# Output stage: the first tile's matmuls walk the 128-row blocks of the weight for both column halves, the second tile's low part is made before the row loads are waited for, and the gate row is loaded by itself

## The reference, cut to what matters

```python
o = jnp.concatenate([o_r, o_h], axis=-1)          # mixer output, 1056 x 1024
mix = o @ W_out                                   # W_out is 1024 x 1024
x = x + gt1 * mix                                 # gate row, one per sequence
h = rmsnorm(x, norm2_g) * (1 + sc2) + sh2         # scale row and shift row
ff = hier_moe(h, ...)                             # router logits of h choose 2 of 16 experts
x = x + gt2 * ff
```

## Time and profile before

| | us |
|---|---|
| median of three runs | 1271.62 |
| the profiled execution, its own time | 1272.07 |
| its span | 1270.3 |
| output stage, from about 656.5 to 832.0 | 175.5 |
| PE busy in that stage | 135.27 |
| DVE busy in that stage | 111.60 |
| ACT busy in that stage | 42.41 |

### The profile page before, as it was taken

How to read it: one execution, slowest core, us unless ns; L and a number is a source line. 1 busy time by engine, 2 the same in 40 slices (tenths; PEclk the granted TensorE clock), 3 DMA queues, 4 the chain that set the end, 5 groups by cost and what they waited for, 6 DMA issues and landing times. The chain is left out here.

```text
span 1270.3 us, 26353 instructions
## 1 busy us (share of the span) xinstructions
PE 1076.6 (85%) x8764; PEld 894.3 (70%) x8765; DVE 717.3 (56%) x1328; ACT 605.9 (48%) x1219; POOL 113.2 (9%) x237
## 2 busy tenths in 40 slices
PE   4689998999989999899948999439999998999800
PEld 4688787977888788877836877337877776777600
DVE  3523555146622565235654675767896684767359
ACT  5634445344543445334551221156786574767334
POOL 0000000000000000000000011220011011111042
PEclk9699999999999999999968999669999999999955
DMA  8532222042122221123225341288999896999175
GB/s 335 183 89 72 77 80 68 26 138 81 38 64 68 80 80 50 44 77 109 80 90 181 101 149 58 75 276 314 373 390 346 303 355 206 375 301 375 70 257 195
DMA packets 202261, 210.63 MB, mean 166 GB/s; under 512 B 15596, under 2 KB 169060, under 8 KB 201892
## 3 DMA queue, kind: packets, MB, share of 16 engines
q1 hardware_dynamic: 182976, 177.25, 41.9%
q0 software_dynamic: 5712, 18.23, 4.1%
q10 hardware_dynamic: 13492, 13.96, 3.1%
HBM read 185.32 MB, written 24.08 MB: 165 GB/s over the span
## 5 line engine op out<-in xcount | busy, mean ns | idle before, releaser
L1998 DVE TENSOR_TENSOR experts_w_lo<-all_raw,experts_w_hi 128x2048 fp32r<-128x2048 f32 x48 | 109.5, 2284 | 6.5 <-ACT experts_w_hi L1879 6.5
L1998 DVE TENSOR_TENSOR experts_w_lo<-experts_raw_more,experts_w_hi 128x2048 fp32r<-128x2048 f32 x48 | 108.3, 2287 | 8.4 <-ACT experts_w_hi L1879 8.4
L908 PE MATMUL early_ps_proj<-mixers_w_hi,early_h_hi 128*128 128x512 f32 x256 | 106.4, 416 | 2.6 <-ACT mixers_decay L741 2.6
L2165 PE MATMUL experts_ps_g<-experts_w_hi,experts_x_hi 128*128 128x512 f32 x256 | 104.4, 408 | 2.2 <-DVE experts_x_lo L2004 2.2
L910 PE MATMUL early_ps_proj<-mixers_w_hi,early_h_lo 128*128 128x512 f32 x256 | 101.1, 395 | 0.0
L2167 PE MATMUL experts_ps_g<-experts_w_hi,experts_x_lo 128*128 128x512 f32 x256 | 100.7, 393 | 0.0
L909 PE MATMUL early_ps_proj<-mixers_w_lo,early_h_hi 128*128 128x512 f32 x256 | 100.6, 393 | 0.0
L2166 PE MATMUL experts_ps_g<-experts_w_lo,experts_x_hi 128*128 128x512 f32 x256 | 100.5, 393 | 0.0
L1198 DVE TENSOR_TENSOR mixers_qd_t<-mixers_turned,early_tables 128x128 f32<-128x128 f32 (+1 forms) x36 | 10.1, 281 | 153.1 <-ACT mixers_turned L789 135.8
L1879 ACT ACTIVATE experts_w_hi<-all_raw 128x2048 fp32r<-128x2048 f32 x48 | 91.5, 1910 | 6.8 <-DMA all_raw<-in_W_up_e_dram 3.5
L1879 ACT ACTIVATE experts_w_hi<-experts_raw_more 128x2048 fp32r<-128x2048 f32 x48 | 91.6, 1913 | 2.2 <-DMA experts_raw_more<-in_W_up_e_dram 1.1
(11 more groups left out here) (354 smaller groups left out, 2757.7 us busy)
## 6 DMA issues: line engine op xcount, KB each, us to landing
experts_raw_more<-in_W_down_e_dram SPq DMA_DIRECT2D x128, 256.0 KB, 5.0
all_raw<-in_W_gate_e_dram SPq DMA_DIRECT2D x96, 256.0 KB, 5.5
all_raw<-in_W_up_e_dram SPq DMA_DIRECT2D x96, 256.0 KB, 6.8
all_raw<-in_W_in_dram SPq DMA_DIRECT2D x32, 512.0 KB, 4.6
all_raw<-in_W_ada_dram SPq DMA_DIRECT2D x32, 512.0 KB, 5.4
condition_w_ada_in<-in_W_ada_dram SPq DMA_DIRECT2D x4, 2048.0 KB, 12.4
experts_raw_more<-in_W_gate_e_dram SPq DMA_DIRECT2D x32, 256.0 KB, 7.2
experts_raw_more<-in_W_up_e_dram SPq DMA_DIRECT2D x32, 256.0 KB, 7.4
```

Source lines behind the costliest of these rows:

```text
L908: pe.matmul(out, xhi, whi, start=(k == 0), stop=False)
L1998: dve.tensor_tensor(w_lo[:, 2 * p:2 * p + 2], raw_pair[p], f32(w_hi[:, 2 * p:2 * p + 2]), ALU.subtract).then_inc(lo_done, 1)
L2165: pe.matmul(out, x_hi[:, k, :], w_hi[:, c, at], start=(k == 0), stop=False)
```

## The change

On SP the load of `o` tile 1 is issued right behind that of tile 0. The gate row of the prompt becomes a load of its own (512 KB) that counts on `x_in[0]`, the semaphore of the even x tiles; the shift and the scale row follow in one load (1024 KB) on `rows_in`. `o` tile 2 and x tile 1 are issued before the tile loop; the sample's rows, with their wait, come behind them. In the loop, the loads of turn 0 are gone, since they were made earlier. On PE, tile 0 takes the blocks k outside and the two column halves inside; all other tiles keep their order. On DVE the low part of tile 1 comes right behind the weights, ahead of the wait for the rows; the making of (1 + scale) * gain, with the wait for `rows_in`, is put behind the x addition of tile 0 for the prompt and behind that of tile 3 for the sample; the wait for the router's loads moves to turn 1, ahead of the first use of the bias.

```diff
             o_tile(0)
-
+            o_tile(1)
             for k in range(6, KD):
                 sp.wait_ge(lo_done, k - 5)
                 sp.dma_start(raw[:, W_OUT_AT[k]], a["W_out"][0, k * P:(k + 1) * P, :])\
                   .then_inc(raw_in[k - 6], 16)
             x_tile(0)
-            o_tile(1)
-            for q, rows in ((0, P), (1, DEC)):
-                if q == 1:
-                    sp.wait_ge(lo_done, KD)
-                sp.dma_start(mod[q][0:rows], s.mod_scr[q:q + 1, 0:3 * D].rearrange("o (c d) -> o c d", c=3)
-                             .broadcast_to([rows, 3, D])).then_inc(rows_in, 16)
+            mod_row = lambda q: s.mod_scr[q:q + 1, 0:3 * D].rearrange("o (c d) -> o c d", c=3)
+            sp.dma_start(mod[0][:, 0:1], mod_row(0)[:, 0:1].broadcast_to([P, 1, D])).then_inc(x_in[0], 16)
+            o_tile(2)
+            sp.dma_start(mod[0][:, 1:3], mod_row(0)[:, 1:3].broadcast_to([P, 2, D])).then_inc(rows_in, 16)
             sp.dma_start(gain[:, :], a["norm2_g"].broadcast_to([P, D])).then_inc(rows_in, 16)
+            x_tile(1)
+            sp.wait_ge(lo_done, KD)
+            sp.dma_start(mod[1][0:DEC], mod_row(1).broadcast_to([DEC, 3, D])).then_inc(rows_in, 16)
...
-                if i + 2 < NT:
+                if 0 < i < NT - 2:
                     o_tile(i + 2)
-                if i + 1 < NT:
+                if 0 < i < NT - 1:
                     x_tile(i + 1)
...
-                for c in range(2):
-                    for k in range(KD):
+                order = [(c, k) for c in range(2) for k in range(KD)] if i else [(c, k) for k in range(KD) for c in range(2)]
+                for c, k in order:
                         if i == 0 and c == 0:
                             pe.wait_ge(lo_done, k + 1)
...
-                    last.then_inc(mm_done, 1)
+                        if k == KD - 1:
+                            last.then_inc(mm_done, 1)
...
-            dve.wait_ge(rows_in, 48)
-            for q, rows in ((0, P), (1, DEC)):
-                last = dve.scalar_tensor_tensor(out=mod[q][0:rows, 2], in0=mod[q][0:rows, 2], scalar=1.0,
-                                                in1=gain[0:rows, :], op0=ALU.add, op1=ALU.mult)
-            last.then_inc(gain_done, 1)
-            dve.wait_ge(gain_done, 1)
-            dve.wait_ge(route_in, 64)
+            o_low(1)
+
+            def norm_rows(q, rows):
+                dve.wait_ge(rows_in, 48)
+                dve.scalar_tensor_tensor(out=mod[q][0:rows, 2], in0=mod[q][0:rows, 2], scalar=1.0,
+                                         in1=gain[0:rows, :], op0=ALU.add, op1=ALU.mult).then_inc(gain_done, 1)
+                dve.wait_ge(gain_done, q + 1)
+
             for i in range(NT):
...
-                if i + 1 < NT:
+                if 0 < i < NT - 1:
                     o_low(i + 1)
+                arrived = 16 * (i // 2 + 1) + (16 if b == 0 else 0)
+                if i == 0:
+                    dve.wait_ge(x_in[0], arrived)
                 dve.wait_ge(mm_done, 2 * i + 2)
...
-                dve.wait_ge(x_in[b], 16 * (i // 2 + 1))
+                dve.wait_ge(x_in[b], arrived)
                 dve.tensor_tensor(x_new, x_new, x_old[0:w, b, :], ALU.add).then_inc(added, 1)
+                if i == 0:
+                    norm_rows(0, P)
+                if i == 3:
+                    norm_rows(1, DEC)
...
+                if i == 1:
+                    dve.wait_ge(route_in, 64)
                 if i:
                     add_bias(i - 1)
```

## The result

The changed kernel takes 1265.87 us (median of 12 runs, 1259.72 to 1269.3), against 1272.1 us (median of 12, 1269.98 to 1274.43) for the kernel before: ratio 0.995, interval 0.9935 to 0.9965, so 4.5 to 8.3 us faster. Forecast was 1264.0, range 1260.8 to 1267.3; within it, both measured medians lie not in the forecast's own 1262.9 to 1265.0 but in rival B's 1265.0 to 1266.3. A second set of six runs gave 1265.46 us and 0.9939 (0.992 to 0.9958). One run of 3719 us (sample rows apart; 1265.99 is the median there without it) and one of 1334.7 us (kernel before) fell in a slower state and are in no ratio.

What follows compares the result with a forecast made beforehand. PE, fullest in the output stage, was taken to idle 5.43 us before tile 1 for its low part; 5.68 plus 2.76 (clock) less 0.80 (new stall) gave 7.64 us, so 1264.0 us, range 1260.8 to 1267.3.

Steps and rivals of the forecast that it cites:

- rival B: Output stage: norm rows 1.0 us late or tile 0's load 1.3 us slower, total 1265.0 to 1266.3; chance 0.10.
- The low part's wait goes with its gap: Between tiles 0 and 1 on PE: earlier low part removes the idle time, tile 1 starting 5.68 us earlier.
- The clock: PE in tile 1: clock no longer falls from 2.4 to 1.2 GHz in the gap, gaining 2.76 us.
- The new stall at the transposes: PE in tile 1, ahead of transposing tile 0's h: a new wait for DVE of 0.80 us.
- the norm row's zero: DVE after tile 0's x addition: prompt's norm row fits in the 1.78 us wait for ACT's root, cost 0.
- D: Rival at the wait for all rows: sample's rows land as late as 687.1, total 1275.1; chance 0.03.
- Order of tile 0: PE in tile 0: blocks outside, column halves inside, so low parts of weights no longer hold it; gain 0.1 us.
- gate row: DVE's gate multiplication of tile 0: the row shares x tile 0's semaphore, both landing ahead of 673.4; cost 0.
- loads moved: SP's queue: tile 1 of o ahead of the last two weight blocks could make them 1.3 us later; cost 0.
- The rest of the stage moves as a whole: Output stage from tile 2 on: PE and DVE wait only for each other, so an earlier tile 2 shifts everything.
- The other sign: Clock at tile 6: with the stage 7.6 us earlier its fall may stay out, total 1262.4; chance 0.10.
- Sum: Whole kernel: -7.64 us against the profiled 1272.07 gives 1264.43, with the median of runs 0.45 us lower 1264.0.

Runs made afterwards that it cites:

- sample rows apart: Changed kernel with the sample's rows counted on the odd x tiles' semaphore, so the prompt's norm row does not wait for them: 1266.26 us, ratio 0.9941.
- The low part alone: Kernel before with one edit, the low part of o tile 1 made ahead of the wait for the rows: 1271.93 us, ratio 0.9989.
- a gap of 2.65 us: Changed kernel with tile 1's low part made only after tile 0's gate multiplication, so PE idles between the tiles without a DMA wait: 1266.71 us, ratio 0.996.
- the old order: Changed kernel with tile 0's column halves outside and blocks inside, as in the kernel before: 1265.54 us, ratio 0.9937.
- the low parts ahead of the choice: Changed kernel with sample's rows on another semaphore, transposes two blocks later, tiles 4 and 6's high and low parts ahead of expert choice: 1258.29 us, ratio 0.9889.
- one row load: Changed kernel with the prompt's three modulation rows in one load again, counted with x tile 0: 1265.36 us, ratio 0.9941.
- filling the wait: Changed kernel with six matmuls that nothing reads put on PE ahead of the waits of tiles 4 and 6: 1265.34 us, ratio 0.9934.
- the changed kernel again: Changed kernel run once more with no edit, for a second profile: 1265.46 us.

## Why the prediction was right, and where its terms were off

- *The low part's wait goes with its gap.* Right in that no profile with the low part right behind the weights has idle time between tiles 0 and 1. But the gap was not what mattered most. The low part alone gained nothing, and with the wait for the rows moved a gap of 2.65 us cost only some 1 us. Seen from h of tile 0: before, it was ready 32.04 us after the stage's start (688.49 and 0.05) and PE came for it at 34.34; in the first profile after, it was ready at 27.30 and PE was waiting. So 4.7 of these 7.0 us are h coming earlier, since the wait for the rows no longer stands ahead of it on DVE, and 2.3 are the gap and the clock. The prediction's sum, 5.68 and 2.76 less 0.80, has the same total and hides this.
- *The clock.* Right in that tile 1 runs at full clock after the change. Its 2.76 us was a term read off one execution; the second profile of the kernel before gives 2.37 (9.32 - 6.95). The runs show the fall to hang on more than the gap's length: 2.65 us idle left the clock up, 1.92 us brought it down late (1.6 us), 5.43 and 5.98 us had it down at once. The Trainium skill (TensorE: Matmul & The Clock Gate, "HAM oscillation — how this bites in real kernels") puts the trouble at idle gaps longer than the 1.5 us of tile 4; the second profile of the changed kernel does not agree, with the clock down after 1.50 us.
- *The new stall at the transposes.* Right in place, mis-sized: 0.80 forecast; 1.09 and 2.75 us measured, and 1.68 with the old order. The term that was wrong is the norm row's zero. It was to hold for a landing by 678.68, 22.2 us after the stage's start, and I took 677.9, 21.4 us. In the five profiles in which the wait was for the sample's rows it ended after 22.7, 23.8, 23.4, 24.2 and 22.8 us; the upper bound was 23.2. The load took 9.9 and 11.0 us from issue to landing in the two profiles of the changed kernel, against 6.4 before. The root's step then starts 0.2 and 1.9 us later than ACT's root alone would have let it (679.15 against 677.17 + 1.78; 678.83 against 675.18 + 1.78). This is rival B, and D's mechanism at a small size. (Two slips in the working change little: the bytes queued up to the prompt's shift row are 4608 KB and not the 4096 KB of before, yet these rows landed 16.6 us after the stage's start, against 16.9 before; and D's 17.8 us should be 18.0.) The division by 398 GB/s was right for most of the bytes and wrong for the tail. The windows of the first profile after (the last two numbers are DMA share and GB/s) have the engines still busy at 674 to 676 us with few bytes moving, and the rows landed only at 677.9:

```profile
672.00:674.00 2.00, 2.00 (x11) 1.65 (x10) 0.00 (x0) 0.00 (x0) 0.00 (x0) 1.00 1.23 406
674.00:676.00 2.00, 2.00 (x11) 1.65 (x10) 1.29 (x2) 0.00 (x0) 0.00 (x0) 1.00 0.88 70
```

  Of the 1694 packets of 674 to 676 us all but 9 are under 512 bytes. The router's weights, 16 and 64 KB in rows of 16 and 64 bytes, are issued right behind the sample's rows, and the division by 398 GB/s leaves them out. That they are what held the rows up is likely by this, but no run moved them. Nor are the sample's rows the only late ones: with them counted elsewhere, in the run with the low parts ahead of the choice, the norm row still waited 0.57 us for the gain row.
- *Order of tile 0, gate row, loads moved.* Costed at 0.1, 0 and 0; the runs with the old order and with one row load agree. The Trainium skill's warning of cycling between PSUM banks (same page, "A second HAM failure mode: psum-queue depth-cycling") did not come true: at alternating banks the matmuls of tile 0 last 0.39 us like the others, once the clock is up.
- *The rest of the stage moves as a whole.* Not quite. "5 to 6" takes about 1 us more in both profiles of the changed kernel (18.5 against 17.5), through a longer fall of the clock at tile 6, which filling the wait removed. It is 18.4 to 18.7 us in six of the seven profiles that have the wait for the rows moved and no help at tile 6 (17.6 with the old order), and 17.35 to 17.6 in all four that have it in its old place. Why an earlier tile 6 should meet a longer fall is open. The other sign, a fall that stays out (1262.4), did not come at tile 6 in any profile of the changed kernel.
- *Sum.* -7.64 forecast; about -6.4 and -7.8 us by the two ratios (0.995 and 0.9939). The stage, where the change acts, is shorter by 5.5 us in the mean of two profiles each. The terms that the prediction put at nothing cost 0.2 to 1.9 us (late rows) and 1 us (clock at tile 6). That the total came within 2 us of the forecast owes something to luck: what is left lies within the 2 us or more by which single executions differ outside the stage.

## What to carry to other kernels

When two waits stand in one engine's program, look for who wants the second one's result: moving one product ahead of a wait pays only if the next consumer is freed too, as the run with the low part alone shows. The run with the 2.65 us gap shows the other side: an idle gap ahead of a tile costs little while the same engine would wait for something else a few us later. A counting semaphore shared by loads makes the first user wait for the last load; give a load that is wanted later to a semaphore that is waited for later. And work that another engine waits for belongs ahead of a long serial chain such as the expert choice: that, with the transposes moved and the sample's rows apart, gave another 7 us.

## What the runs showed that was not expected

The length of a wait did not decide whether the granted clock fell. Behind the same wait of 1.48 to 1.50 us ahead of tile 4 it fell in eight profiles ("3 to 4" of 16.6 to 16.9 us) and stayed up in three (15.8 us); the kernel before and the changed kernel each gave one profile of either kind. Between two streams of 128x512 matmuls it stayed up over 2.65 us and fell, late, after 1.92 us; it stayed up too over the stalls of 2.75 and 2.78 us at tile 0's transposes (the changed kernel again, one row load). The waits at tiles 4 and 6 come behind 1.85 and 1.96 us of matmuls with 20 columns; behind the same 20-column matmuls without a wait, ahead of tiles 3 and 5, the clock stayed up. No fall came at tiles 4 and 6 in the two kernels in which dense matmuls followed the 20-column ones at once. At the stage's start, 6 to 14 matmuls ran at the lower clock before it rose, which alone moves tile 0's end by up to 1.5 us from one profile to another (gate multiplication after 18.7 to 20.3 us where it waits for PE).
